# The experts' normed input, 32 bytes further on in its buffer

## The reference

```python
h = rms_norm_2(x, ffn_norm_gain[layer])
x = x + peer_ffn(h, peer_w_q[layer], peer_sub_keys[layer], peer_u[layer], peer_v[layer])
# peer_ffn, for a block of 128 tokens xb:
q = (xb @ w_q).reshape(PEER_BLOCK, PEER_HEADS, 2, PEER_HALF)
scores = jnp.einsum('thpd,hpkd->thpk', q, sub_keys)
top_s, top_i = lax.top_k(scores, PEER_TOPK)      # then the best 16 of 16 x 16 sums, per head
act = jax.nn.gelu(jnp.einsum('thkd,td->thk', u[expert], xb), approximate=False)
return jnp.einsum('thk,thkd->td', gate * act, v[expert])
```

## Time and profile before

| | us |
|---|---|
| median of 3 executions | 2181.78 |
| lowest, highest | 2173.94, 2183.56 |
| the profiled execution's own time | 2181.81 |
| its span in the trace | 2180.5 |
| TensorE busy, matmuls | 2111.7 |
| VectorE busy | 1532.0 |
| ScalarE busy | 1104.6 |
| mean granted TensorE clock, as a share of full speed | 0.978 |

### The profile page before, as it was taken

How to read it: one execution, slowest core, us unless ns; L and a number is a source line. 1 busy time by engine, 2 the same in 40 slices (tenths; PEclk the granted TensorE clock), 3 DMA queues, 4 the chain that set the end, 5 groups by cost and what they waited for, 6 DMA issues and landing times.

```text
span 2180.5 us, 33874 instructions
## 1 busy us (share of the span) xinstructions
PE 2111.7 (97%) x13326; PEld 1848.2 (85%) x13326; DVE 1532.0 (70%) x2626; ACT 1104.6 (51%) x1765; POOL 185.8 (9%) x102
## 2 busy tenths in 40 slices
PE   7997999999999999889999899999999999999999
PEld 6886789888888888668888678999999999888887
DVE  5667675766676667856666676898889995555555
ACT  5554633265555555555554875545444444444443
POOL 0000013300011000110003003243000000000000
PEclk9999999899999999899999899999999999999999
DMA  6566221166655665236665325545544445565554
GB/s 196 185 193 203 80 87 68 52 182 191 187 172 183 190 188 181 93 99 193 192 188 200 108 96 185 174 158 184 173 144 146 146 146 184 193 193 193 193 193 155
DMA packets 97629, 352.45 MB, mean 162 GB/s; under 512 B 10896, under 2 KB 12688, under 8 KB 97088
## 3 DMA queue, kind: packets, MB, share of 16 engines
q1 hardware_dynamic: 97472, 350.29, 50.1%
HBM read 349.20 MB, written 1.05 MB: 161 GB/s over the span
## 4 chain that ended last, share of the span: by engine, by line
PE 87%; DVE 7%; ACT 3%; issue 1%; POOL 1%; DMA 0%; SPq 0%; ACTq 0%; DVEq 0%
PE psum L268 19%; PE psum L269 18%; PE psum L270 18%; PE psum L312 15%; PE psum L311 6%; PE psum L2732 2%; DVE tile_low L204 1%; PE psum L873 1%; PE psum L315 1%; ACT tile_high L192 1%; PE psum L1070 1%; PE psum L354 1%; POOL small L1688 1%; PE psum L950 1%; DVE peer_active L2939 0%
## 5 line engine op out<-in xcount | busy, mean ns | idle before, releaser
L204 DVE TENSOR_TENSOR tile_low<-raw_tiles,tile_high 128x1024 fp32r<-128x1024 f32 x598 | 741.1, 1241 | 379.1 <-ACT tile_high L192 373.1
L192 ACT ACTIVATE tile_high<-raw_tiles 128x1024 fp32r<-128x1024 f32 x642 | 677.1, 1056 | 423.2 <-PE psum L270 418.7
L312 PE MATMUL psum<-hT,tile_high 128*128 128x512 f32 x1408 | 494.3, 396 | 5.2 <-issue 5.2
L311 PE MATMUL psum<-hT,tile_low 128*128 128x256 f32 x1232 | 344.2, 279 | 0.0
L268 PE MATMUL psum<-hT,tile_high 128*128 128x256 f32 x1152 | 334.3, 290 | 2.6 <-DVE tile_low L204 2.3
L268 PE MATMUL psum<-tile_high,hT 128*128 128x512 f32 (+1 forms) x816 | 324.1, 397 | 4.4 <-DVE hT L2081 1.8
L269 PE MATMUL psum<-hT,tile_high 128*128 128x256 f32 x1152 | 327.7, 284 | 0.0
L270 PE MATMUL psum<-hT,tile_low 128*128 128x256 f32 x1152 | 327.4, 284 | 0.0
L269 PE MATMUL psum<-tile_low,hT 128*128 128x512 f32 (+1 forms) x816 | 320.3, 393 | 0.0
L270 PE MATMUL psum<-tile_high,hT 128*128 128x512 f32 (+1 forms) x816 | 319.8, 392 | 0.0
L312 PEld LDWEIGHTS psum<-hT,tile_high 128*128 128x128 f32 x1408 | 258.6, 188 | 54.5 <-issue 5.6
(11 more groups left out here) (365 smaller groups left out, 2657.7 us busy)
## 6 DMA issues: line engine op xcount, KB each, us to landing
raw_tiles<-ffn_in_dram SPq DMA_DIRECT2D x176, 512.0 KB, 3.6
raw_tiles<-peer_u_dram SPq DMA_DIRECT2D x128, 512.0 KB, 3.3
raw_tiles<-peer_v_dram SPq DMA_DIRECT2D x128, 512.0 KB, 4.3
raw_tiles<-ffn_out_dram SPq DMA_DIRECT2D x88, 512.0 KB, 3.5
raw_tiles<-w_kv_dram SPq DMA_DIRECT2D x16, 512.0 KB, 3.4
raw_tiles<-in_gates_dram SPq DMA_DIRECT2D x16, 512.0 KB, 3.3
raw_tiles<-peer_q_dram SPq DMA_DIRECT2D x16, 512.0 KB, 3.5
raw_tiles<-w_k_dram SPq DMA_DIRECT2D x8, 512.0 KB, 3.6
```

What stands on the lines that cost most here:

```text
L192: scalar.activation(k.high[:, n % SLOTS, :], k.raw[:, n % RAW_SLOTS, :], ACT.Copy).then_inc(*k.tile_high_made.mark(n))
L204: vector.tensor_tensor(k.low[:, n % SLOTS, :], k.raw[:, n % RAW_SLOTS, :], k.high[:, n % SLOTS, :].bitcast(F32), ALU.subtract).then_inc(*k ...
L311: k.tensor.matmul(ps[:, 0:T], low[:, c, :], both[:, c, 0, :], start=False, stop=False, skip_group_check=True)
L312: ins = k.tensor.matmul(ps, high[:, c, :], both[:, c, :, :], start=(c == 0), stop=(c == KC - 1), skip_group_check=True)
```

## The change

`hT` becomes a buffer that is 16 values (64 bytes) longer. The old view `k.hT` stays on its beginning. A second view of the same shape, `k.h_between`, begins 8 values (32 bytes) further on. The experts' normed input is written and read through the second view; everything else, the second half's parts too, uses the first. All buffers that are allocated behind `hT` (the raw and split tiles, `cols` and all the rooms) move by 64 bytes.

```diff
+LINE = 16
@@ tensor_peer
     for g in range(PAIRS):
         ps = bank(k, ("peer_u", g), k.weighed if waiting(g) else k.activated, ("pair", g))
         for i in range(2):
-            feature_major(k, ps[:, i * T:(i + 1) * T], k.hT, normed if (g, i) == (0, 0) else None,
+            feature_major(k, ps[:, i * T:(i + 1) * T], k.h_between, normed if (g, i) == (0, 0) else None,
                           chunks_passed if (g, i) == (PAIRS - 1, 1) else None)
@@ scalar_peer
-        scalar.activation(k.hT[0][:, chunks, :], r["whole"][:, chunks, :], ACT.Copy).then_inc(
+        scalar.activation(k.h_between[0][:, chunks, :], r["whole"][:, chunks, :], ACT.Copy).then_inc(
             *k.h_high_made.mark(("peer", "normed", half)))
@@ vector_peer
-        vector.tensor_tensor(four_chunks(half, k.hT[1]), four_chunks(half, r["whole"]),
-                             four_chunks(half, k.hT[0]).bitcast(F32), ALU.subtract).then_inc(
+        vector.tensor_tensor(four_chunks(half, k.h_between[1]), four_chunks(half, r["whole"]),
+                             four_chunks(half, k.h_between[0]).bitcast(F32), ALU.subtract).then_inc(
                                  *k.h_low_made.mark(("peer", "normed", half)))
@@ program
-    k.h_both = sb("hT", [P, KC, 2, T], F32R)
+    spread_out = sb("hT", [P, 2 * KC * T + LINE], F32R)
+    k.h_both = spread_out[:, 0:2 * KC * T].rearrange("p (c n t) -> p c n t", n=2, t=T)
     k.hT = (k.h_both[:, :, 0, :], k.h_both[:, :, 1, :])
+    between = spread_out[:, LINE // 2:LINE // 2 + 2 * KC * T].rearrange("p (c n t) -> p c n t", n=2, t=T)
+    k.h_between = (between[:, :, 0, :], between[:, :, 1, :])
```

## The result

The changed kernel takes 2185.06 us (median of 14 executions, 2178.8 to 2192.65), the kernel before, run beside it, 2181.31 us (14 executions, 2173.37 to 2183.56). The ratio is 1.0025, 95% interval 1.0013 to 1.0036: slower by a quarter of a per cent, where I had forecast 4 us less. The profiled execution took 2185.38 us, its span is 2184.1 us, 3.6 more than before.

What follows compares the result with a forecast made beforehand. TensorE, busy 97% of the span, was taken as the bound through its matmuls' pace; gains of 1.7, 2.2 and 0.4 us sum to 4.3, taking 2181.8 to 2177.5 us, range 2171 to 2186.

Steps and rivals of the forecast that it cites:

- The pace of the first half: Matmuls of L2761 in the experts' first half: 118.3 ns instead of 120.0; L2714's score matmuls 9.42 us apart.
- The gain of the first half: Experts' first half, matmuls of L2761: 1.67 or 1.4 ns less each, 4.3 us in all.
- The stretch of the lots: 64 tiles of the first half with L2732's matmuls between: 1.4 ns less per matmul, 2.2 us.
- The wait for VectorE: TensorE's wait for `tile_low` during VectorE's sorting: grows from 2.3 to 2.7 us, taking the gain of 10 tiles.
- The writers of the view: L2791 and L2897 write the shifted buffer, hidden by 23 us of `peer_q` matmuls: even a doubling costs nothing.
- the clock behind the wait: TensorE returns from the wait at 1.2 GHz; one such spell, lost or spared, is 1.4 us, only in the range.
- VectorE's room in the lots' stretch: VectorE, busy 214.57 of 236.00 us there, keeps over 19 us idle and does not become the limit: no cost.
- The buffers behind `hT`: Tiles and rooms move 64 bytes against `hT`, every start staying on a multiple of 64: taken as 0.
- The third rival: The tiles' 64-byte move matters in other stages reading `hT`: 16 us less 4.3 gained, 2194; could also help; chance 0.07.
- The first rival, the layout: Separate buffers against `hT`'s side-by-side halves, not the place, set the first half's pace: no gain, 2181.8 us; chance 0.17.
- The second: Rival: the 32 bytes cost the first half up to 6.6 ns per matmul, 18.7 us, 2200; chance 0.05.

Runs made afterwards that it cites:

- the map: Kernel before with hT read at shifts of 0 to 496 bytes in 16-byte steps, no buffer moved, results not the reference's; 113.3 to 120.0 ns at 256 columns.
- rooms_32: Kernel before with only cols 32 bytes longer, so the rooms behind it come onto the tiles' multiple; 2178.8 us, ratio 0.9981.
- longer_128_at_32: The change with hT's buffer 128 bytes longer instead of 64, the first half still reading 32 bytes on; 2185.9 us, ratio 1.0036 against the kernel before.
- place 112: Kernel before with the first half's view 144 bytes before hT, the pad ahead of hT, and minus_half 32 bytes shorter; 2167.0 us, ratio 0.9943.

## Why the prediction was wrong

- The pace of the first half was right: 118.3 ns forecast, 118.4 measured, and 9.42 us for three tiles with scores, 9.41 measured. That was luck in part. I placed the view 32 bytes off with "the tiles still on it", but it got `peer_first`'s own place, 224, only because the tiles moved by 64 as well; at 32 the map has 116.8.
- The gain of the first half was nearly right, 4.3 us forecast and 3.4 in the profile. The stretch of the lots gave 1.6 of its 2.2 us, and 0.3 went into a wait of the transposes for VectorE.
- The wait for VectorE was right: forecast 2.7, measured 2.5 us, with the gain of the ten tiles ahead of it lost.
- The writers of the view took what they had taken (1.05, 1.22 and 2.36 us) and the clock behind the wait cost nothing new, 3.4 us at the lower level in both, as forecast. VectorE's room in the lots' stretch cost nothing either.
- The step that failed is "The buffers behind `hT`", which I took at 0, "since all rows show one difference only". The rows could not show it. Every pair in the rows was at 0 or 224 modulo 256, so they fixed the pace at two places and said nothing of the period. I took 64 bytes as the period because 0 and 32 past 64 was the shortest description. I also misread the rooms: they are not 32 but 96 bytes past a multiple of 128 (94,048, for one), 32 short of the next. The term was worth +7 us in the profile, +3.5 ahead of the first half and +3.5 behind it, and it outweighed the −3.4. The part behind is firm: the second half takes 348.0 or 348.1 us in the seven profiles with `hT` at 0, 351.4 in both at 192, 356.8 in both at 128. Of the part ahead only the first matrices' 5.4 us are firm.
- The third rival had the mechanism, with 0.07. Its price, 16 us for 2448 matmuls at 6.6 ns, was too high, because 192 costs the 512-column matmuls 2.2 ns and not 6.6, and its sum left out the first matrices, which were the largest item.
- The first rival, the layout, falls with the map and with rooms_32. The second falls too, for the first half: place 224 costs 512-column pairs and serves 256-column ones.
- The range held the median, 2185.06 within 2171 to 2186, but that was luck: its upper end stood for a case without effect plus scatter. The ratio says slower, and I had it faster.

What stays open is why. It could be that the read of the next weights and that of the moving operand meet. The weight load's own duration seemed to hint at it: in the first half its median is 192 ns before and 188 after; here the row of the kernel before:

```profile
L268 PEld LDWEIGHTS psum<-hT,tile_high x1024: 187/192/334, 1401.8 to 1827.7; 128*128 128x128 f32 x171
```

But the load does not follow the pace elsewhere. In the second half of the kernel before, at 226.7 ns, its median is 188, and in that of longer_128_at_32, at 232, it is 188 too. No run separated the load of the next weights from the running matmul, so the cause is open.

## What to carry to other kernels

When a buffer grows, everything behind it moves, and operands that nobody edited get another place against each other; put a pad so that only the intended pair moves, or count every pair that it shifts. Two places seen in a trace say how those two run and nothing of the period between; one kernel that reads at many shifts gives the map. And a matmul stream that is made faster in a stage with other work meets the next engine: with place 112 the waits grew from 2.3 to 8.9 us, and the time at the lower clock behind them from 3.4 to 10.2.

## What the runs showed of the hardware that was not expected

- The distance between float32r matmuls with a weight load each depends on the moving operand's address minus the stationary one's. Measured in steps of 16 bytes it is 113.3 to 120.0 ns at 256 columns and 226.7 to 234.4 at 512. At 512 columns the map repeats after 256 bytes to 0.1 ns, at 256 columns to 1.3. The two shapes have different good places: 512 columns are fastest within 16 bytes of 0 (226.7), and 256 columns are slowest at 0 and 96 (120.0).
- At some places (64, 192) the distance takes one of two values, 113.3 or 117.7 ns, by how a stream is entered. The pace of matmuls that nothing touches can change with what precedes them: in rooms_32 the first matrices entered from the second ones run at 354 ns a pair and the others at 347, 2.4 us in all.
